# Twenty-four more projection units stream both parts of the tokens in one product, and VectorE adds the two sums

## The reference, cut to what matters

```python
# each of the two layers
proj = rmsnorm(x) @ w_in          # mqk, mv, mo, gates, aq, ak, av, ga, gb
scores = einsum(q, k_ctx) * (A_HEAD_DIM ** -0.5)
y = sigmoid(ga) * (hm @ w_branch_m) + sigmoid(gb) * (ha @ w_branch_a)
...
# second block
q_a, k_a, v_a, q_b, k_b, v_b, gate_a, gate_b = split(rmsnorm(h) @ w_in)
y_a = merge(moba_attention(q_a, k_a, v_a)) @ w_out_moba
y_b = merge(stick_breaking_attention(q_b, k_b, v_b)) @ w_out_sb
h = h + (sigmoid(gate_a) * y_a + sigmoid(gate_b) * y_b) @ w_mix_out
h = h + peer_ffn(rmsnorm(h), ...)
```

## Time and profile before

| | us |
|---|---|
| median of 3 runs (lowest, highest) | 1725.02 (1724.77, 1725.88) |
| profiled execution, own time | 1725.26 |
| its span in the profile | 1723.5 |
| PE busy in the span | 1598.0 |
| DVE busy | 1171.3 |
| ACT busy | 861.0 |

### The profile page before, as it was taken

The page is one execution under the profiler, slowest core; times in us unless marked ns, Lnnn a source line. Parts: engine busy times, 40 slices in busy tenths (PEclk is TensorE's granted clock), DMA queues, the critical chain, the costliest instruction groups (busy, mean ns, idle before and its releaser), DMA issues.

```text
span 1723.5 us, 21303 instructions
## 1 busy us (share of the span) xinstructions
PE 1598.0 (93%) x8114; PEld 1172.0 (68%) x8114; DVE 1171.3 (68%) x2057; ACT 861.0 (50%) x1565; POOL 357.6 (21%) x383
## 2 busy tenths in 40 slices
PE   9999999999999999999999999999987787877776
PEld 8988998888998899888889997555422222322222
DVE  6758766666775876666665567987666667766745
ACT  5556544443465554434455545655544454444443
POOL 0200000000120000000060101644634444343440
PEclk9999999999999999999999999999999999999999
DMA  8443554555544355555534367999999999999996
GB/s 315 170 147 126 197 192 175 192 191 183 195 159 150 139 196 188 190 182 189 195 147 147 147 218 303 404 421 422 421 422 421 421 422 421 422 421 421 421 421 278
DMA packets 67800, 464.97 MB, mean 270 GB/s; under 512 B 7529, under 2 KB 9713, under 8 KB 12786
## 3 DMA queue, kind: packets, MB, share of 16 engines
q0 software_dynamic: 37152, 268.45, 37.6%
q1 hardware_dynamic: 30256, 194.83, 31.3%
q10 hardware_dynamic: 290, 0.33, 0.1%
HBM read 462.53 MB, written 1.06 MB: 269 GB/s over the span
## 4 chain that ended last, share of the span: by engine, by line
PE 62%; DMA 23%; DVE 7%; issue 4%; ACT 3%; POOL 1%; POOLq 0%; ACTq 0%
PE acc L625 13%; PE acc L627 13%; PE acc L626 13%; DMA arena<-in_peer_uv,arena 12%; PE att L650 5%; DMA row_w_lo<-in_peer_uv,arena 5%; DMA row_xa<-in_peer_uv,arena 3%; PE acc L650 3%; PE att L651 3%; PE acc L1799 3%; DMA row_w_hi<-in_peer_uv,arena 2%; PE acc L1802 2%; PE acc L651 1%; DVE w_lo L587 1%; DVE arena L2312 1%
## 5 line engine op out<-in xcount | busy, mean ns | idle before, releaser
L587 DVE TENSOR_TENSOR w_lo<-arena,w_hi 128x2048 fp32r<-128x2048 f32 x170 | 388.2, 2294 | 158.2 <-ACT w_hi L580 157.8
L580 ACT CAST w_hi<-arena 128x2048 fp32r<-128x2048 f32 x174 | 331.6, 1907 | 119.1 <-PE acc L627 98.7
L1941 ACT ACTIVATE arena<-arena,small 128x1 f32<-128x1 f32 x256 | 75.2, 294 | 279.7 <-DVE arena L2312 128.0
L2312 DVE SCALAR_TENSOR_TENSOR arena<-arena 128x1024 f32<-128x1024 f32 x122 | 149.1, 1222 | 85.3 <-DMA arena<-in_peer_uv,arena 81.0
L625 PE MATMUL acc<-xa,w_hi 128*128 128x256 f32 x672 | 192.0, 286 | 0.4 <-DVE w_lo L587 0.4
L626 PE MATMUL acc<-xa,w_lo 128*128 128x256 f32 x672 | 190.1, 283 | 0.0
L627 PE MATMUL acc<-xa,w_hi 128*128 128x256 f32 x672 | 190.0, 283 | 0.0
L1799 PE MATMUL acc<-arena,gate_raw 128*128 128x512 f32 x244 | 133.2, 628 | 53.8 <-ACT gate_raw L1951 50.3
L2554 POOL DMA_INDIRECT arena<-in_peer_uv,arena x122 | 132.3, 1084 | 174.4 <-PE acc L1802 138.4
L650 PE MATMUL att<-xa,w_hi 128*128 128x512 f32 x384 | 136.0, 398 | 0.0
L625 PE MATMUL acc<-w_hi,xb 128*128 128x512 f32 (+1 forms) x336 | 130.3, 388 | 2.3 <-DVE xb L771 1.8
(11 more groups left out here) (351 smaller groups left out, 3482.9 us busy)
## 6 DMA issues: line engine op xcount, KB each, us to landing
arena<-in_units SPq DMA_DIRECT2D x174, 1024.0 KB, 4.8
arena<-in_units SPq DMA_DIRECT2D x4, 512.0 KB, 5.3
arena<-in_bias SPq DMA_DIRECT2D x1, 2048.0 KB, 9.4
arena<-in_peer_uv,arena POOLq DMA_INDIRECT x122
x_res<-in_x SPq DMA_DIRECT2D x2, 512.0 KB, 5.8
arena<-m_parked SPq DMA_DIRECT2D x2, 512.0 KB, 3.9
arena<-in_norm_mlp_g SPq DMA_DIRECT2D x2, 512.0 KB, 6.7
arena<-in_norm_g SPq DMA_DIRECT2D x2, 512.0 KB, 5.8
```

Of the source, the lines that this page charges most:

```text
L580: nc.scalar.copy(w_hi[:, s, :], raw[HOME[g]]).then_inc(S["hi_ready"], 1)
L587: nc.vector.tensor_tensor(w_lo[:, s, :], raw[HOME[g]], w_hi[:, s, :].bitcast(F32), ALU.subtract).then_inc(S["lo_ready"], 1)
L2312: nc.vector.scalar_tensor_tensor(row, row, 1.0, hn[:, n // SLOTS, :], ALU.mult, ALU.mult, accum_out=dots[:, n:n + 1]).then_inc(S["rows_use ...
```

## The change

Eight `aq` units (four in each layer) and sixteen units of the second block (qa, ka, qb, kb, two each; ga2, gb2, four each) go from `unit_f` to `unit_wide`. Each now fills two banks, so the bank tables are new. Of the 24 units DVE adds the sums of 22 with a `tensor_reduce` of 128x1024 numbers from PSUM; for the two `qa` units ACT scales one half out of PSUM and DVE adds the other with a `scalar_tensor_tensor`. The factor of `aq` moves to `ak`, that of `qb` into the sigmoids' scale. The sigmoid of the gates stays on ACT but reads what DVE has written, in place, and waits for it.

```diff
@@ layers
-            BANKS["aq", i] = [acc[i]]
+            BANKS["aq", i] = acc[0:2] if i % 2 == 0 else acc[2:4]
...
-                    if name in ("ga", "gb") or name == "up" and i >= 4:
+                    if name in ("aq", "ga", "gb") or name == "up" and i >= 4:
                         unit_wide(b, s, xa, ("u", u), between)
...  layer_act, take
-                elif name == "aq":
-                    unit(name, i)
-                    nc.scalar.mul(aq[:, 2 * i:2 * i + 2, :], b[0][:].rearrange("p (n t) -> p n t", n=2), A_DH ** -0.5).then_inc(
-                        S["emptied_act"], mark("emptied_act", (name, i)))
...  layer_dve, take
+                if name == "aq":
+                    unit(name, i)
+                    both = acc_banks[:, 0:2, :] if i % 2 == 0 else acc_banks[:, 2:4, :]
+                    nc.vector.tensor_reduce(aq[:, 2 * i:2 * i + 2, :], both.rearrange("p n (c t) -> p n t c", c=2), X, ALU.add).then_inc(
+                        S["emptied_dve"], mark("emptied_dve", (name, i)))
@@ second block
-            BANKS["ga2", i] = BANKS["gb2", i] = [acc[i]]
+            BANKS["ga2", i] = BANKS["gb2", i] = acc[0:2] if i % 2 == 0 else acc[2:4]
...
+        WIDE2 = {"qa", "ka", "qb", "kb", "ga2", "gb2"}
+        BY_DVE2 = {"yab", "mix"} | WIDE2
...  second_pe
-                    if kind == "F":
-                        unit_f(b, s, xh, xl, ("u", u), between=between)
+                    if name in WIDE2:
+                        unit_wide(b, s, xa, ("u", u), between)
...  second_act, take
-                if name in ("qa", "qb"):
+                if name == "qa":
                     unit(name, i)
-                    q = qa if name == "qa" else qb
-                    nc.scalar.mul(q[:, 2 * i:2 * i + 2, :], two, DH2 ** -0.5).then_inc(
+                    nc.scalar.mul(qa[:, 2 * i:2 * i + 2, :], acc_banks[:, 2:4, 0:SEQ], DH2 ** -0.5).then_inc(
                         S["emptied_act"], mark("emptied_act", (name, i)))
-                elif name in ("ka", "kb"):
-                    unit(name, i)
-                    k_ = ka if name == "ka" else kb
-                    nc.scalar.copy(k_[:, 2 * i:2 * i + 2, :], two).then_inc(S["emptied_act"], mark("emptied_act", (name, i)))
...
                 elif name in ("ga2", "gb2"):
-                    unit(name, i)
-                    g = ga if name == "ga2" else gb
-                    nc.scalar.activation(g[:, 2 * i:2 * i + 2, :], two, ACT.Sigmoid).then_inc(
+                    g = (ga if name == "ga2" else gb)[:, 2 * i:2 * i + 2, :]
+                    act.wait_ge(S["emptied_dve"], at("emptied_dve", (name, i)))
+                    nc.scalar.activation(g, g, ACT.Sigmoid).then_inc(
                         S["emptied_act"], mark("emptied_act", (name, i)))
...  second_dve, take
+                if name in WIDE2:
+                    into = {"qa": qa, "ka": ka, "qb": qb, "kb": kb, "ga2": ga, "gb2": gb}[name][:, 2 * i:2 * i + 2, :]
+                    both = acc_banks[:, 2:4, :] if b[0] is acc[2] else acc_banks[:, 0:2, :]
+                    if name == "qa":
+                        dve.wait_ge(S["emptied_act"], at("emptied_act", (name, i)))
+                        nc.vector.scalar_tensor_tensor(into, both[:, :, SEQ:2 * SEQ], DH2 ** -0.5, into, ALU.mult, ALU.add).then_inc(
+                            S["emptied_dve"], mark("emptied_dve", (name, i)))
+                    else:
+                        unit(name, i)
+                        nc.vector.tensor_reduce(into, both.rearrange("p n (c t) -> p n t c", c=2), X, ALU.add).then_inc(
+                            S["emptied_dve"], mark("emptied_dve", (name, i)))
```

More of the change, by code:

```diff
@@ L834, in build @@
             BEFORE["up", i] = [("up", 2), ("up", 3)] if i == 4 else [("up", i - 2)]
-        BY_ACT = {"mqk", "mv", "aq", "av"}
+        BY_ACT = {"mqk", "mv", "av"}
         SCORED_AFTER = {("mo", 1): 0, ("mo", 3): 1, ("ga", 1): 2, ("ga", 3): 3}
@@ L1374, in take @@
                 b = BANKS[name, i]
-                if name == "ak":
+                if name == "aq":
[3 more added lines that the diff above has]
+                        S["emptied_dve"], mark("emptied_dve", (name, i)))
+                elif name == "ak":
                     unit(name, i)
@@ L1381, in take @@
                             last = (odd, half) == (1, 1)
-                            nc.vector.tensor_copy(ak[64 * half:64 * half + 64, odd::2, :], ps).then_inc(
+                            nc.vector.tensor_scalar(ak[64 * half:64 * half + 64, odd::2, :], ps, A_DH ** -0.5, None, ALU.mult).then_inc(
                                 S["emptied_dve" if last else "ak_part"], mark("emptied_dve" if last else "ak_part", (name, i) if last else (odd, half)))
@@ L1607, in build @@
         for i in range(2):
-            BANKS["qa", i], BANKS["ka", i], BANKS["qb", i], BANKS["kb", i] = [acc[2 - 2 * i]], [acc[3 - 2 * i]], [acc[2 + i]], [acc[i]]
+            BANKS["qa", i], BANKS["ka", i] = acc[2:4], acc[0:2]
+            BANKS["qb", i] = BANKS["kb", i] = acc[2:4] if i == 0 else acc[0:2]
             BANKS["va", i], BANKS["vb", i] = acc[0:2], acc[2:4]
         for i in range(4):
-            BANKS["ga2", i] = BANKS["gb2", i] = [acc[i]]
+            BANKS["ga2", i] = BANKS["gb2", i] = acc[0:2] if i % 2 == 0 else acc[2:4]
             BANKS["yab", i] = acc[2 * (i % 2):2 * (i % 2) + 2]
@@ L1615, in build @@
             BANKS["pq", i] = [acc[i % 2]]
-        BEFORE2 = {("qa", 1): [("va", 0)], ("ka", 1): [("va", 1)], ("qb", 0): [("qa", 0)], ("qb", 1): [("ka", 0)],
[3 rows of a table removed]
+        BEFORE2 = {("ka", 0): [("va", 1)], ("qa", 1): [("qa", 0)], ("ka", 1): [("ka", 0)], ("qb", 0): [("qa", 1)], ("qb", 1): [("ka", 1)],
+                   ("kb", 0): [("qb", 0)], ("kb", 1): [("qb", 1)], ("vb", 0): [("kb", 0)], ("ga2", 0): [("kb", 1)], ("ga2", 1): [("vb", 1)],
+                   ("yab", 0): [("gb2", 2)], ("yab", 1): [("gb2", 3)],
                    ("yab", 2): [("yab", 0)], ("yab", 3): [("yab", 1)], ("mix", 0): [("yab", 2)], ("mix", 2): [("yab", 3)],
                    ("pq", 0): [("mix", 0)], ("pq", 1): [("mix", 1)]}
-        for i in range(4):
-            BEFORE2["gb2", i] = [("ga2", i)]
+        for i in range(2):
+            BEFORE2["ga2", 2 + i], BEFORE2["gb2", i], BEFORE2["gb2", 2 + i] = [("ga2", i)], [("ga2", 2 + i)], [("gb2", i)]
         for i in range(2, 8):
@@ L1628, in build @@
         row_sums = [acc[2:4], acc[0:2]]
-        BY_DVE2 = {"yab", "mix"}
+        WIDE2 = {"qa", "ka", "qb", "kb", "ga2", "gb2"}
+        BY_DVE2 = {"yab", "mix"} | WIDE2
         def emptied2(eng, name, i):
@@ L1875, in weights @@
                     for e in range(2):
-                        nc.scalar.activation(stay[:, e, :], att[e][:, 0:384], ACT.Sigmoid, scale=-1.0).then_inc(
+                        nc.scalar.activation(stay[:, e, :], att[e][:, 0:384], ACT.Sigmoid, scale=-DH2 ** -0.5).then_inc(
                             S["odds"], mark("odds", (p, e, 0)))
-                        nc.scalar.activation(stop[:, e, :], att[e][:, 0:384], ACT.Sigmoid).then_inc(
+                        nc.scalar.activation(stop[:, e, :], att[e][:, 0:384], ACT.Sigmoid, scale=DH2 ** -0.5).then_inc(
                             S["odds"], mark("odds", (p, e, 1)))
@@ L2137, in take @@
                 b = BANKS[name, i]
-                if name == "yab":
+                if name in WIDE2:
[9 more added lines that the diff above has]
+                            S["emptied_dve"], mark("emptied_dve", (name, i)))
+                elif name == "yab":
                     unit(name, i)
```

## The result

The changed kernel takes 1733.15 us, the median of 6 runs (1732.45 to 1735.14), against 1724.95 for six runs of the kernel before (1724.44 to 1725.88) on the same chip. The ratio is 1.0046, with a 95% interval of 1.0036 to 1.0056: slower by 0.46%, and an interval that ends well above 1. The forecast was 1733.4. The profiled execution took 1732.45 us, the lowest of the six, and its span is 1730.7.

What follows compares the result with a forecast made beforehand. PE was taken to bound the kernel up to the PEER layer, but an ACT-DVE round to bind at the gates. -0.96 - 0.32 + 9.56 = +8.3 us gave 1733.4 us, 0.5% slower, range 1728.5 to 1737.

Steps and rivals of the forecast that it cites:

- The gates: Units ga2 and gb2, second block: a closed round through ACT and DVE outlasts PE's 14.04 us round, costing +9.56 us.
- The three rounds: From step 4's first sigmoid to step 7's, stick-breaking: 13.41, 14.28 and 14.27 us become 16.79 each.
- the last piece: From step 7's first sigmoid to the first yab unit: 13.28 us becomes 14.43, so +1.15.
- The ten pieces of the sum: ACT and DVE durations and hand-overs from one stick-breaking step's first sigmoid to the next's, together 16.79 us.
- q and k: Eight second-block units: 0.96 us saved, first scores 0.64 us later for ka0's reduction, together -0.32 us.
- the third rival: Steps 1 to 3: DVE's additions delay the logits, up to 1.22 us each, +3.7, total 1737.1; chance 0.07.
- aq: Eight units in the layers: wide products save 0.12 us each with DVE's reductions hidden, -0.96 us.
- The Trainium skill's rule: Fixed cost per PE product about 2.5 ns: sixteen units outside the gates save 0.6 us, not 1.9; sum 1.3 higher.
- The sum: Whole kernel: aq, q and k, and gates together +8.3 us.
- Nothing is exposed: Rival, whole change: 2.9 us saved less 0.64 for the first scores, total 1722.8; chance 0.05.
- The round binds less: Rival, gates: first reduction and sigmoid (1.78 us) drop out, round 15.0, 7.1 us less, total 1726.3; chance 0.05.

Runs made afterwards that it cites:

- sigmoids_late: The changed kernel with the gates' sigmoids made as two of 128x2048 behind units gb2 2 and gb2 3, DVE's additions kept: 1722.24 us, ratio 0.9980.
- hi_first: The changed kernel, but at each even gate unit ACT does the next unit's `split_hi` before the gate's sigmoid, nothing removed: 1722.87 us, ratio 0.9986.
- gates_by_copy: The kernel before, all products unchanged, but DVE copies each gate unit out and ACT's sigmoid waits for that copy: 1731.10 us, ratio 1.0033.
- gates_back: The changed kernel with gates ga2 and gb2 put back as before; aq, q and k stay wide: 1722.82 us, ratio 0.9984.
- aq_only: The kernel before with only the layers' aq wide and added on DVE, its factor moved to `ak`: 1723.74 us, ratio 0.9992.
- gates_only: The changed kernel with aq, q and k put back as before, only the eight gate units wide: 1736.45 us, ratio 1.0062.

## Why the prediction was right

**The gates: right, in place, mechanism and size.** +9.56 predicted, +9.50 measured (953.68 to 1018.42 is 64.74, less 55.24). The three rounds came within 0.02 us of 16.79, the last piece within 0.04 of 14.43. The ten pieces of the sum, read off the round above, are 3.38, 3.21, 2.20, 1.25, 0.54, 1.91, 2.21, 1.26, 0.54 and 0.30, each within 0.02 of what the sum had. The mechanism is shown, not only argued: with all of DVE's added work and ACT's list reordered no round exceeds 14.19 (`sigmoids_late`, `hi_first`); with nothing of the change but the hand-over, the rounds grow to 15.72 (`gates_by_copy`). The releasers are those named: ACT before DVE's `split_lo`, DVE before ACT's gate sigmoid. PE's wait before `product`, forecast as 2 to 3 us, was 2.15, 1.28, 2.66 and 2.69; the 1.28 is taken up in the last section.

**q and k: right.** The first scores wait 1.32 us for DVE, forecast 1.3. From qa0 to step 4's first sigmoid it took 70.44 us (883.24 to 953.68) against 70.86 (884.52 to 955.38): -0.42, forecast -0.32. That the two agree to 0.1 is as much as can be said. `gates_back`, `sigmoids_late` and `hi_first` have the same code there and took 70.65, 70.67 and 70.64, a gain of only 0.19 to 0.22. The 0.2 between them is in qa0 and ka0: a pair of products takes 0.347 us there in the changed kernel and 0.353 in the other three. The logits behind an addition are not late. DVE around one of them in the changed kernel:

```profile
909.00 1.23 DVE L2144 TENSOR_REDUCE arena<-acc 128x512 f32<-128x1024 f32 x1 [1.53 <-PE acc L651]
910.96 0.29 DVE L2089 CUSTOM_DVE_ANT_0 arena<-att,arena 128x128 f32<-128x128 f32 x1 [0.73 <-PE att L1673]
```

Behind the addition DVE still waits 0.73 us for PE's scores. That is the margin of the third rival, which had 3.65 us before: it did not happen, but not by much.

**aq: right sign, wrong size.** The step that was mis-sized is "8 x 0.12 = 0.96". Measured are 1.75 in the changed kernel (26.07 and 26.06) and 1.74 in `aq_only`. The row that gave 0.12 is of units in an undisturbed sequence. In the first layer of the changed kernel aq0 saved just that, 0.10 (5.75 to 5.65). aq1, cut in two by the gate's columns, went from 6.05 to 5.80 without these, the small products between aq1 and aq2 (L898, L899) from 1.34 to 1.23, aq2 from 5.84 to 5.64 and aq3 from 5.76 to 5.55. With 0.01 at the gate's columns this adds up to 0.88 a layer.

Two things are in it. A wide pair of products, which takes 0.353 us in aq0 (5.65 over 16 pairs), takes 0.347 in aq2 and aq3 (5.55 over 16), while three narrow products take 0.360 wherever nothing interrupts them (5.76 over 16). And there is less lost where one kind of product gives way to another: from the start of aq1's last product to the first small one it is 0.22 before (72.31 to 72.53) and 0.11 after (72.41 to 72.52). What the small products ahead cost at the start of aq2, 0.09 us, is the same in both forms (the first product takes 0.21 in place of 0.12, and 0.32 in place of 0.23), so it is no part of the saving. Why a wide pair has two speeds at a granted clock of 1.00, and which one it will show, stays open. The trace of before has the faster one too: in the second layer's last gb units eight pairs from 607.90 take 0.346 each. One pair of `up` units could not show that.

The Trainium skill's rule of about 2.5 ns of fixed cost per product (TensorE: Matmul & The Clock Gate, "Wait — 56ns, not 53.3ns?") would give 0.32 us for 128 products less. The stretches show 1.74 to 1.75, some 13.7 ns per product removed. Where nothing interrupts a unit it is 7 ns at the slower pair (0.360 less 0.353) and 13 at the faster. The trace decides, and my choice of the row over the rule erred on the same side, only less.

**The sum.** -1.75 - 0.42 + 9.50 = +7.33, where I had +8.3. The spans differ by 7.2. The rest is at no place that the edits are known to touch: +0.47 before and between the aq stretches, of which 0.35 is PE's wait for the first load (2.62 us, 2.27 before), and -0.60 behind the first yab unit, 712.9 us before and 712.3 after. Over the nine traces that last stretch lasted from 711.6 to 713.4. In the three kernels that come to it late (1016.5 to 1020.6) it took 711.6, 712.3 and 713.2, in the other six 711.9 to 713.4, so beyond this scatter what the gates cost is not given back in the PEER layer. The medians are 8.2 apart. That the forecast of 1733.4 met 1733.15 within 0.3 us is partly luck: the aq term was off by 0.8, and the 0.9 by which the medians exceed the sum of the traced parts has no cause that the traces show. The six runs alone spread over 2.7 us.

**Rivals.** "Nothing is exposed", 1722.8, is what `sigmoids_late` took (1722.24): the saving exists, once the round does not bind. "The round binds less" fell with the rounds of 16.8 us. `hi_first` is the kernel in which its condition holds, an addition and a sigmoid off ACT's way to `split_hi`; its round is 14.19, under the 15.0 that I gave the rival. I had taken out the addition and the sigmoid (1.78 us) only; with them goes the second `split_hi` (1.93), for DVE then runs `split_lo`, addition, `split_lo`, addition without a wait for ACT. So more than its 7.1 us was at stake: the kernel with its condition took 1722.87 and not 1726.3.

## What to carry to other kernels

When work moves from one engine to another, look at who then waits for whom: if A waits for B in the middle of A's list, and what stands behind that wait feeds B, the two form a round, and its length is at least the sum of the pieces of both engines on that way, however idle each looks in the average. Write that round down piece by piece from the trace and compare it with the round of the engine that bounds the kernel; here 16.79 against 14.04 us settled it. The cure is not less work but order: put what the other engine needs ahead of the instruction that waits for it, which turned this change from +0.46% into -0.14%, or take the waiting instruction out of the round, which gave -0.20%.

## What the hardware showed beside that

After PE's first long wait its clock fell to half. PE in the changed kernel before and during step 5's unit (from left to right: the stretch, its length, the busy us of PE, PEld, DVE, ACT and POOL with their instructions, the granted clock, the DMA share, GB/s):

```profile
965.00:967.00 2.00, 0.00 (x0) 0.01 (x1) 0.85 (x1) 1.88 (x3) 0.00 (x0) 1.00 0.78 328
967.00:968.00 1.00, 0.98 (x12) 0.90 (x12) 1.00 (x1) 0.00 (x0) 0.00 (x0) 1.00 0.00 0
968.00:969.00 1.00, 1.00 (x10) 0.64 (x8) 1.00 (x2) 0.00 (x0) 0.00 (x0) 0.72 0.06 16
969.00:970.00 1.00, 1.00 (x5) 0.55 (x3) 0.58 (x1) 0.39 (x1) 0.00 (x0) 0.50 0.36 98
970.00:971.00 1.00, 1.00 (x5) 0.90 (x4) 0.00 (x0) 1.00 (x5) 0.00 (x0) 0.50 0.95 319
971.00:972.00 1.00, 1.00 (x6) 0.81 (x5) 0.00 (x0) 1.00 (x4) 0.00 (x0) 0.58 1.01 410
972.00:975.00 3.00, 3.00 (x20) 2.62 (x18) 1.17 (x3) 1.89 (x2) 1.49 (x4) 1.00 0.18 74
```

PE did nothing from 965 to 967, worked, and from about 968.4 to 971.8 was granted 0.50, the level of 1.2 GHz; a pair of products took 0.64 us (970.16 to 970.80) in place of 0.35. Then it was back at 1.00. The next wait before `product` shows what PE lost by it: 1.28 us, where the two that follow take 2.66 and 2.69, so by my estimate 1.4 us. The round it fell in lasted 16.80 us like the others. PE was slowed by 1.4 us inside a round and the round did not grow, so PE does not set it. `gates_only` shows the same twice: its granted clock was 0.79 over 967 to 975 and 0.83 over 1000 to 1010, PE's waits behind these falls are 1.29 and 1.10 us in place of 2.7, and the rounds are 16.8 us all the same.

The wait of 2.65 us in `gates_only` (up to 1002.82) was followed by a fall, the wait of 2.66 us at the same place of the changed kernel (up to 1000.60) by none. The length of the wait before alone doesn't tell whether the clock falls; what else does stays open here.
